# Small float32 products of a chunked recurrence, split into halves of 32 weight columns on four column groups

## What is computed

```python
def wkv_scan(state0, r, decay, kk, b, v, k, reverse):
    def step(S, inp):
        r_t, w_t, kk_t, b_t, v_t, k_t = inp
        sa = jnp.einsum("bhvk,bhk->bhv", S, kk_t)
        S = (S * w_t[:, :, None, :] - sa[..., None] * b_t[:, :, None, :]
             + v_t[..., None] * k_t[:, :, None, :])
        return S, jnp.einsum("bhvk,bhk->bhv", S, r_t)
```

## Time and profile before

| | us |
|---|---|
| median of 3 runs | 1660.35 |
| lowest, highest | 1658.63, 1661.67 |
| the profiled execution: span, first to last instruction | 1657.6 |
| TensorE busy (matmul) | 1571.5 |
| TensorE weight loads | 1324.2 |
| VectorE busy | 885.0 |
| ScalarE busy | 572.7 |
| GpSimd busy | 219.5 |

### The profile page before, as it was taken

The page is one execution under the profiler, slowest core; times in us unless marked ns, Lnnn a source line. Parts: engine busy times, 40 slices in busy tenths (PEclk is TensorE's granted clock), DMA queues, the critical chain, the costliest instruction groups (busy, mean ns, idle before and its releaser), DMA issues.

```text
span 1657.6 us, 36556 instructions
## 1 busy us (share of the span) xinstructions
PE 1571.5 (95%) x15540; PEld 1324.2 (80%) x15540; DVE 885.0 (53%) x1417; ACT 572.7 (35%) x987; POOL 219.5 (13%) x230
## 2 busy tenths in 40 slices
PE   7899998999999978999999999999979999999997
PEld 3787886999999766778777887777867788888886
DVE  1624213665566445888887224667454556555222
ACT  3422334332232223434443223535544222323221
POOL 0000002333233010111111121000001011111111
PEclk8899997999999988999999998999979999999999
DMA  8242100332210121222222232221102222222221
GB/s 340 77 147 77 51 26 8 99 106 92 81 42 4 53 77 52 98 79 102 101 81 107 88 104 76 82 79 57 46 26 98 80 93 86 100 101 95 90 102 68
DMA packets 38750, 139.74 MB, mean 84 GB/s; under 512 B 3040, under 2 KB 3552, under 8 KB 38112
## 3 DMA queue, kind: packets, MB, share of 16 engines
q1 hardware_dynamic: 38480, 135.76, 23.4%
q10 hardware_dynamic: 144, 2.10, 0.3%
HBM read 135.75 MB, written 2.10 MB: 83 GB/s over the span
## 4 chain that ended last, share of the span: by engine, by line
PE 86%; DVE 8%; ACT 3%; issue 1%; DMA 0%; POOL 0%; DVEq 0%; SPq 0%; ACTq 0%
PE bank L647 58%; PE bank L780 12%; DVE ffn_sb L2471 2%; PE bank L657 2%; PE bank L967 1%; PE bank L610 1%; PE bank L886 1%; PE bank L908 1%; PE bank L888 1%; PE bank L592 1%; PE bank L1285 1%; PE bank L910 1%; ACT arena L1752 1%; DVE w_in L2091 1%; PE bank L1256 1%
## 5 line engine op out<-in xcount | busy, mean ns | idle before, releaser
L647 PE MATMUL bank<-hf_hi,w_up 128*128 128x512 f32 x1376 | 424.9, 390 | 0.0
L647 PEld LDWEIGHTS bank<-hf_hi,w_up 128*128 128x128 f32 x1376 | 259.1, 188 | 53.6
L647 PE MATMUL bank<-hf_lo,w_up 128*128 128x512 f32 x688 | 271.2, 394 | 4.8 <-DVE w_up L2091 4.3
L647 PE MATMUL bank<-act_hi,w_down 128*128 128x512 f32 x704 | 216.8, 389 | 0.0
L780 PE MATMUL bank<-arena 64*64 64x32 f32 (+2 forms) x4992 | 177.0, 227 | 8.5 <-POOL arena L1930 7.6
L780 PEld LDWEIGHTS bank<-arena 64*64 64x64 f32 x4992 | 170.6, 137 | 13.2 <-issue 8.7
L1403 ACT ACTIVATE w_up<-ring 128x1024 fp32r<-128x1024 f32 x88 | 93.0, 1058 | 215.9 <-PE bank L647 215.9
L2091 DVE TENSOR_TENSOR w_up<-ring,w_up 128x1024 fp32r<-128x1024 f32 x88 | 108.0, 1229 | 105.3 <-ACT w_up L1403 105.2
L647 PEld LDWEIGHTS bank<-hf_lo,w_up 128*128 128x128 f32 x688 | 129.5, 188 | 39.4 <-DVE w_up L2091 13.2
L2471 DVE SCALAR_TENSOR_TENSOR ffn_sb<-ffn_sb 128x512 f32<-128x512 f32 x176 | 151.5, 861 | 5.5
L647 PEld LDWEIGHTS bank<-act_hi,w_down 128*128 128x128 f32 x704 | 132.2, 188 | 27.4
(11 more groups left out here) (319 smaller groups left out, 2364.8 us busy)
## 6 DMA issues: line engine op xcount, KB each, us to landing
ring<-w SPq DMA_DIRECT2D x76, 1024.0 KB, 4.7
ring<-w SPq DMA_DIRECT2D x32, 704.0 KB, 4.0
ring<-w SPq DMA_DIRECT2D x64, 256.0 KB, 2.9
arena<-w SPq DMA_DIRECT2D x2, 3072.0 KB, 22.6
x<-xT SPq DMA_DIRECT2D x1, 2048.0 KB, 11.8
arena<-w SPq DMA_DIRECT2D x2, 1024.0 KB, 20.3
x<-xT ACTq DMA_DIRECT2D x1, 2048.0 KB, 8.9
outT<-x SPq DMA_DIRECT2D x4, 512.0 KB, 2.7
```

The costliest lines, as they stand in the source:

```text
L647: ins = mm(out, w[:, a, k, :], of_block(b, k0 + k), start=first and k == 0 and m == 0, stop=last and k == n - 1 and m == 2)
```

## The change

`QUADS` lists, for each half of the partitions r and each half c of the 64 weight columns, the rows r, the partitions of the output (`to`) and the weight columns. Each product of a half is issued as two products with 32 weight columns and the same moving operand; the four products of a pair of heads write the four groups of 32 partitions, in the order 0-31, 64-95, 32-63, 96-127. Semaphores, buffers and the order of the steps stay. All other products of the kernel stay as they are.

```diff
--- before.py
+++ after.py
@@ -477,6 +477,8 @@
             return a.rearrange("p j (b e s) -> p (j b) e s", e=2, s=1 << l - 1)[:, :, e, :]
 
         HALVES = (slice(0, HD), slice(HD, P))
+
+        QUADS = tuple((r, slice(r.start + c, r.start + c + 32), slice(c, c + 32)) for c in (0, 32) for r in HALVES)
 
         bank = [banks[0:4], banks[4:8]]
 
@@ -776,8 +778,8 @@
             def tiles(out, lhs, rhs):
 
                 for j in range(NJ):
-                    for r in HALVES:
-                        last = mm(out(j, r), lhs(j, r), rhs(j, r), start=True, stop=True)
+                    for r, to, c in QUADS:
+                        last = mm(out(j, to), lhs(j, r)[:, c], rhs(j, r), start=True, stop=True)
                 return last
 
             def kk_spread(j):
@@ -882,10 +884,10 @@
                 v_in = v_tok[:, place(d, n) // L]
                 for j in range(NJ):
                     out = bank[d][3][:, L * j:L * j + L]
-                    for r in HALVES:
-                        mm(out[r], sc.ktrt[r, n % 3, j, 0:L], sc.S[r, n % 2, j, :], start=True, stop=False)
-                    for r in HALVES:
-                        last = mm(out[r], sc.kr[r, n % 2, j, 0:L], v_in[r, j, :], start=False, stop=True)
+                    for r, to, c in QUADS:
+                        mm(out[to], sc.ktrt[r, n % 3, j, c], sc.S[r, n % 2, j, :], start=True, stop=False)
+                    for r, to, c in QUADS:
+                        last = mm(out[to], sc.kr[r, n % 2, j, c], v_in[r, j, :], start=False, stop=True)
                 last.then_inc(s[f"gu_mm{d}"], 1)
 
             def updates(n, d):
@@ -904,10 +906,10 @@
                 v_in = v_tok[:, place(d, n) // L]
                 for j in range(NJ):
                     out = bank[d][3][:, L * j:L * j + L]
-                    for r in HALVES:
-                        mm(out[r], sc.tok[r, 0, j, :], sc.gu[r, j, :], start=True, stop=False)
-                    for r in HALVES:
-                        last = mm(out[r], sc.tok[r, 1, j, :], v_in[r, j, :], start=False, stop=True)
+                    for r, to, c in QUADS:
+                        mm(out[to], sc.tok[r, 0, j, c], sc.gu[r, j, :], start=True, stop=False)
+                    for r, to, c in QUADS:
+                        last = mm(out[to], sc.tok[r, 1, j, c], v_in[r, j, :], start=False, stop=True)
                 last.then_inc(s[f"ds_mm{d}"], 1)
 
             def results(n, d):
@@ -919,12 +921,12 @@
                 v_in = v_tok[:, place(d, n) // L]
                 for j in range(NJ):
                     out = bank[d][0][:, L * j:L * j + L]
-                    for r in HALVES:
-                        mm(out[r], sc.S[r, n % 2, j, :], sc.ktrt[r, n % 3, j, L:2 * L], start=True, stop=False)
-                    for r in HALVES:
-                        mm(out[r], v_in[r, j, :], sc.kr[r, n % 2, j, L:2 * L], start=False, stop=False)
-                    for r in HALVES:
-                        last = mm(out[r], sc.gu[r, j, :], sc.nr[r, n % 2, j, L:2 * L], start=False, stop=True)
+                    for r, to, c in QUADS:
+                        mm(out[to], sc.S[r, n % 2, j, c], sc.ktrt[r, n % 3, j, L:2 * L], start=True, stop=False)
+                    for r, to, c in QUADS:
+                        mm(out[to], v_in[r, j, c], sc.kr[r, n % 2, j, L:2 * L], start=False, stop=False)
+                    for r, to, c in QUADS:
+                        last = mm(out[to], sc.gu[r, j, c], sc.nr[r, n % 2, j, L:2 * L], start=False, stop=True)
                 last.then_inc(s[f"y_mm{d}"], 1)
 
             def nx(m, d, l):
```

## The result

The changed kernel takes **1864.88 us** (median of 4 runs, 1863.7 to 1867.34), the kernel before 1660.86 us (median of 4, 1658.63 to 1661.67) on the same chip. The ratio is 1.1241, 95% interval 1.1215 to 1.1267: slower by 204 us. The forecast was 1866 in 1815 to 1920.

A forecast was written before the change was run, and what follows sets the result against it. The prediction took TensorE to bound the recurrence, and after the change its instruction fetch: 127.4 packets x 3.75 us = 478 us for 274.6, +203, and +3 at the ends, gave 1863.6; plus 2.75 for the median, 1866 us, range 1815 to 1920.

The forecast's parts named there:

- TensorE sets the recurrence's time, and VectorE's work stays covered: Recurrence: TensorE busy 273.5 of 274.6 us is its chain; VectorE, ScalarE and GpSimd have enough time beside it.
- Array time: Recurrence products: halving gains 42 to 50 us at 32 moving columns, nothing at 64 (about 14 ns, twice) or 128.
- Instructions: Recurrence: 15442 TensorE records double, 16594 become 32036, so 66 instruction packets become 127.4.
- A packet's price: Recurrence: starved TensorE gets one instruction packet per 1.25 + 2.5 = 3.75 us (3.4 to 4.2); 478 us, +203.
- the 3 us for the ends: Outside the recurrence stretch: a few hundred changed records at its two ends count as one packet more, +3 us.
- Ends and other stages: Stages before 240 us and behind the recurrence keep their lengths; weights for the next stages stay covered, 0.
- The 0 for L780: Stretch 240 to 274.5 us: 384 L780 records lie between long products, cost 0, at most 6 us.
- The signs: q8 packets 104 to about 167, issue idleness over 200 us, recurrence holes 1.5 to 2.7 us, turn about 42 us.
- Rival 1, half clock: Recurrence: idling TensorE may lose half its clock; packets of 128-column products take 6.9 us, +38 us: 1904; chance 0.13.
- starved at full clock: Main case, recurrence: TensorE waits for instruction packets at full clock, 1866 us; chance 0.67.
- Rival 2, faster: Recurrence: the instruction fetch keeps up and only the array counts, bounded by VectorE, -33 us: 1627; chance 0.08.
- Rival 3, half starved: Recurrence: starved TensorE requests the next packet at once, 2.5 us a packet, +44 us: 1707; chance 0.09.

The follow-up runs named there:

- experiment 1: Kernel before with unused whole and halved products added ahead of the recurrence, looped and written out; 48 halved bursts written out took 43.0 us, 48 whole ones 22.5 us.
- experiment 3: Changed kernel with only the first half of the weight columns, half of every recurrence result left out; 1644.57 us, ratio 0.9908 to the kernel before.
- experiment 5: Kernel before with few products halved: the two scores alone, 1675.3 us, ratio 1.0091; dx of the last level alone, 1666.99 us, ratio 1.0027.
- experiment 2: Kernel before with unused halved products added ahead of the recurrence in four loops of 1280 to 5120 records; second loop 72.2 us, 5120 records 75.5 us a pass.

## Why the prediction held, point by point

- **TensorE sets the recurrence's time, and VectorE's work stays covered.** Right: VectorE is busy for 172.3 us (168.8 before) in a stretch 207.9 us longer, and TensorE's matmuls wait for it there for 1.9 us in all.
- **Array time.** 8 to 9 ns for 32 moving columns: 8.0 in experiment 1. The gain of 42 to 50 us exists only on the array: with the instructions held at their number, and twice the saving, the kernel gained 15 us (experiment 3). The 14 ns for 64 moving columns was interpolated, and it came: in the timeline after, groups of eight follow each other every 0.11 us (681.31 and 681.42). With 128 moving columns, the 64 matmuls of L789 in experiment 5 take 1.95 us with some 0.27 of tail: 26 ns, as taken from L967.
- **Instructions.** 32036 records and 127.4 packets were forecast for the recurrence; 32047 and 126 came, and in all 167, as forecast.
- **A packet's price.** 3.75 us was taken, 3.4 and 4.2 the bounds; 3.83 in the recurrence, 3.58 in experiment 1 and 3.77 to 3.85 in the refetched loops of experiment 2. Both of its parts came. In the recurrence after, a packet starts 1.36 us after a resumption and TensorE resumes 2.47 us after its start (means of 111 holes over 0.6 us), for 1.25 and 2.5. The sum was 478 us where 482.5 stand in the trace, +203 against +207.9; the 3 us for the ends did not come (0.8 and 1.9 us less, not more). The two misses nearly cancel, which makes the total closer than its terms.
- **Why that price.** "TensorE holds two packets, a new one is asked for when the older is used up" failed in its first half: it holds more than 1280 instructions. What fits the starved rows is that one packet is asked for at a time and takes 3.5 to 3.85 us from one to the next, where the array needs less; this is inferred from the packets' times, as no run changes how they are asked for. For this kernel, which never goes back, both readings give one number, so the forecast did not suffer; for a loop they differ widely (experiment 2).
- **Ends and other stages.** The stage up to the recurrence ends 0.8 us earlier, though its 384 records of L780 doubled, and what follows is 1.9 us shorter. The 0 for L780 there held.
- **The signs.** Holes up to 2.5 us, a resumption every 3.7 to 4.0, a turn of 42.6 us (from the first L888 of one turn, at 681.31, to that of the next, at 723.95) for a forecast 42: right. "Over 200 us" of issue idleness was too much by this view: TensorE's idle time in the recurrence is 174.5 us, since the modelled tail of a matmul, some 0.2 us, covers the start of each hole.
- **Rival 1, half clock.** Its condition came: the granted clock is 0.82 in the recurrence, about a third of it at 0.5. The case that was given 0.67, starved at full clock, is thus not quite what happened. The price of the rival, +38, did not come: between packet starts lie on average 3.79 us where the clock was full throughout (58 intervals) and 3.69 where it was half throughout (21), and none is longer than 4.67, where 6.9 was forecast for packets of 128 moving columns.
- **Rival 2, faster.** Excluded: experiment 1 shows that the fetch cannot keep up with 8 ns.
- **Rival 3, half starved.** Excluded by every packet interval read: none of the mean intervals is under 3.46 us, and the shortest single one between packet starts in the recurrence is 3.22.

Two stretches at half clock and three at full clock of the changed kernel:

```profile
288.20:301.80 13.60, 9.87 (x420) 8.90 (x419) 4.90 (x17) 4.00 (x11) 4.92 (x7) 0.50 0.31 92
336.00:349.60 13.60, 9.63 (x429) 9.11 (x431) 4.35 (x14) 1.15 (x3) 0.15 (x1) 0.50 0.27 83
417.90:445.20 27.30, 14.09 (x875) 12.92 (x871) 9.83 (x28) 3.93 (x12) 2.04 (x3) 1.00 0.14 43
503.20:527.10 23.90, 13.69 (x857) 12.53 (x849) 10.16 (x29) 3.33 (x11) 1.32 (x2) 1.00 0.17 48
650.00:667.00 17.00, 8.71 (x628) 8.07 (x630) 4.96 (x14) 3.84 (x10) 6.87 (x10) 1.00 0.02 5
```

31 matmuls start per us at half clock and 35 at full clock (849 in 27.2 us, 2360 in 68.2). A count like this depends on where the stretches are cut: one of 13.6 us holds three or four packets, and half a packet more or less at its ends changes it by some 14%. The intervals between packets, which have no such ends, show none. A packet of the narrowest halved products takes 1.93 us of array at half clock (experiment 1) and fits under the fetch; TensorE only waits less.

What stays open: why resumptions are now 3.46 and now 4.0 us apart (the mean time from a packet to its resumption is 2.47 us in the recurrence and 2.45 in the long loops of experiment 2; it is the delay before the next packet that differs, 1.36 against 1.17); and how much of the +14 and +5 us of experiment 5 is the change of tile size and how much the packets.

## What to carry to other kernels

Where code is written out and products are small, count instructions before array time: here a block of 256 TensorE instructions costs at least 3.5 to 3.8 us, so in a dense run a float32 product (four instructions) below some 55 to 60 ns gains nothing by being faster, and splitting it in two doubles its price. A loop body of 1280 instructions was held after its first pass and escapes this; one of 1792 did so only in part. Keep products of one tile size together: each change cost some 0.17 us at full clock.

## What was not expected of the hardware

- The buffer of TensorE holds between 1280 and 2304 instructions (1792 in part), yet a starved written-out stream gets only one packet of 256 in some 3.5 to 3.85 us, with data transfers beside it or without.
- Satisfied waits between small products are dear: 5888 of them cost 565 us, 96 ns each, and 87 ns where the clock was full.
- A product of another tile size starts some 0.17 us later than one of the same size. Alternating 64x64 and 64x32 tiles took 224 us where the same products in groups of eight took 46.2, a part of it through the clock, which fell to 0.51 while TensorE was counted busy all the time.
- The end of a loop's pass costs about 0.41 us beside halved products and nothing visible beside whole ones.
